# Expert layer in a hybrid decoder step: eight equal expert jobs become four pairs of a 192-slot and a 128-slot job

## The reference

```python
logits = einsum('btd,de->bte', h, w_router) + b_router
top_p, top_i = lax.top_k(softmax(logits), 2)
gates = sum(one_hot(top_i, 8) * (top_p / sum(top_p))[..., None], axis=-2)
for e in range(8):
    y = y + gates[..., e:e+1] * ((silu(h @ wg[e]) * (h @ wu[e])) @ wd[e])
```

## Time and profile before

| | |
|---|---|
| runs | 1703.96 us median of 3 (1699.91 to 1707.03) |
| profiled execution | span 1699.4 us from the first to the last instruction; the page gives no other time of it |
| TensorE busy | 1592.8 us (94%) |
| VectorE, ScalarE, POOL busy | 945.8, 756.0, 540.5 us |
| DMA | 282 MB, mean 166 GB/s |
| expert jobs | eight, from about 1046 to 1678 us of the span |

### The profile page before, as it was taken

The page is one execution under the profiler, slowest core; times in us unless marked ns, Lnnn a source line. Parts: engine busy times, 40 slices in busy tenths (PEclk is TensorE's granted clock), DMA queues, the critical chain, the costliest instruction groups (busy, mean ns, idle before and its releaser), DMA issues.

```text
span 1699.4 us, 29575 instructions
## 1 busy us (share of the span) xinstructions
PE 1592.8 (94%) x11452; PEld 1480.1 (87%) x11452; DVE 945.8 (56%) x1248; ACT 756.0 (44%) x1068; POOL 540.5 (32%) x333
## 2 busy tenths in 40 slices
PE   6998878999999999899888988999999999999998
PEld 5997758999999999898866778989989898989886
DVE  6896554411111000512498349777768686867777
ACT  6444453322222222423586326455545554545455
POOL 1001323254455444143000314614233232415172
PEclk8998879999999999999999998999999999999989
DMA  6624202245444642221764355896969798796961
GB/s 209 132 86 148 83 1 75 73 132 153 128 130 154 199 158 93 68 82 52 255 185 151 105 124 163 284 265 210 298 196 297 198 271 224 234 260 222 257 232 52
DMA packets 346287, 282.01 MB, mean 166 GB/s; under 512 B 9513, under 2 KB 311133, under 8 KB 346071
## 3 DMA queue, kind: packets, MB, share of 16 engines
q1 hardware_dynamic: 324963, 251.09, 50.6%
q10 hardware_dynamic: 18084, 18.14, 3.2%
q0 software_dynamic: 3168, 11.80, 2.4%
HBM read 246.62 MB, written 35.10 MB: 166 GB/s over the span
## 4 chain that ended last, share of the span: by engine, by line
PE 79%; DVE 11%; issue 4%; ACT 4%; DMA 1%; POOL 1%; SPq 1%; ACTq 0%; DVEq 0%; POOLq 0%
PE ps L2452 35%; PE ps L3044 14%; PE ps L3047 6%; PE ps L2438 3%; PE ps L2439 3%; PE ps L2440 3%; PE ps L3071 2%; PE ps L3070 2%; DVE cT L1701 2%; PE ps L2591 2%; DVE wlo L1576 1%; PE ps L2420 1%; DVE ewl L2249 1%; PE ps L2968 1%; PE ps L2477 1%
## 5 line engine op out<-in xcount | busy, mean ns | idle before, releaser
L3044 PE MATMUL ps<-ejx,ewh 128*128 128x384 f32 x1408 | 401.7, 359 | 4.8 <-DVE ejx L2263 1.9
L2249 DVE TENSOR_TENSOR ewl<-eraw,ewh 128x2048 fp32r<-128x2048 f32 (+1 forms) x144 | 304.2, 2113 | 152.8 <-ACT ewh L1418 150.9
L1418 ACT ACTIVATE ewh<-eraw 128x2048 fp32r<-128x2048 f32 (+1 forms) x144 | 255.2, 1773 | 252.7 <-PE ps L3047 145.1
L3047 PE MATMUL ps<-ejx,ewl 128*128 128x192 f32 x1408 | 352.5, 250 | 0.0
L2452 PE MATMUL ps<-hh,whi 128*128 128x260 f32 x1504 | 311.2, 288 | 18.4 <-DVE hl L1951 12.7
L2452 PE MATMUL ps<-hh,wlo 128*128 128x260 f32 x1504 | 306.9, 286 | 0.0
L2452 PE MATMUL ps<-hl,whi 128*128 128x260 f32 x1504 | 306.8, 286 | 0.0
L925 POOL TENSOR_TENSOR ea<-eat,ea 128x128 fp32r<-128x128 f32 x88 | 171.5, 1948 | 340.2 <-ACT ea L1476 339.9
L3044 PEld LDWEIGHTS ps<-ejx,ewh 128*128 128x128 f32 x1408 | 264.2, 188 | 8.4 <-issue 7.0
L3047 PEld LDWEIGHTS ps<-ejx,ewl 128*128 128x128 f32 x1408 | 268.9, 191 | 0.0
L2452 PEld LDWEIGHTS ps<-hh,whi 128*128 128x128 f32 x1504 | 237.1, 192 | 22.0 <-issue 15.9
(11 more groups left out here) (451 smaller groups left out, 2498.5 us busy)
## 6 DMA issues: line engine op xcount, KB each, us to landing
eraw<-in_w_gate_e SPq DMA_DIRECT2D x88, 512.0 KB
eraw<-in_w_up_e SPq DMA_DIRECT2D x88, 512.0 KB
eraw<-in_w_down_e SPq DMA_DIRECT2D x64, 512.0 KB
eraw<-in_w_down_e SPq DMA_DIRECT2D x48, 256.0 KB
xs<-zero ACTq DMA_DIRECT2D x10, 1152.0 KB, 4.8
raw<-in_w_gate_d SPq DMA_DIRECT2D x22, 512.0 KB, 4.0
raw<-in_w_up_d SPq DMA_DIRECT2D x22, 512.0 KB, 5.2
raw<-in_w_down_d SPq DMA_DIRECT2D x16, 512.0 KB, 4.5
```

The costliest lines, as they stand in the source:

```text
L1418: e.activation(ewh[:, s, 0:n], eraw[:, u % RAW, 0:n], ACT.Copy).then_inc(ew_hi, 1)
L2249: e.tensor_tensor(ewl[:, s, 0:n], eraw[:, u % RAW, 0:n], ewh[:, s, 0:n].bitcast(F32), ALU.subtract)\
L3044: e.matmul(ps[:, q, 0:2 * C], ewh[:, s, o:o + P], ejx[:, k, :, :].rearrange("p h n -> p (h n)"), start=(k == 0), stop=(k == KD - 1), skip_ ...
L3047: ins = e.matmul(ps[:, q, C:2 * C], ewl[:, s, o:o + P], ejx[:, k, 0, :], start=False, stop=(k == KD - 1), skip_group_check=True)
```

## The change

The experts are ordered by count. The four largest get "wide" jobs of 192 slots, the four smallest "slim" jobs of 128 slots; a wide and a slim one form a pair, and the slots of a pair are 320 rows of `xs` and `ys`. The loop now runs over pairs. The pair order is wide, slim; the last pair runs slim, wide. If a count exceeds its capacity, more pairs are appended. A wide job works as before. A slim job has the 128 tokens stationary in gate and up too and moves the weights, 256 columns of gate and 256 of up for four k-tiles per unit; its hidden values come out with the tokens on the partitions and are turned by TensorE in six blocks of 256 columns (the last of 128). VectorE makes the low parts of those too (POOL has only the wide jobs' ones). The weights of the first job are loaded once the largest expert is known. Cut to its core:

```diff
-MAXJOBS = (2 * T + E * C) // C
+PAIR = C + P
+BIG = E // 2
+MAXP = BIG + 6
+        LATE = {4: KE - 1, 5: KE}
+        POOL_LOW = ()
+        def turn_block(u):
+            return next((b for b in range(BLOCKS) if u == LATE.get(b, 2 * b + 3)), None)
+        def done_block(u):
+            return u // 2 - 1 if u % 2 == 0 and 2 <= u <= 10 else BLOCKS - 1 if u == KE else None
 # SP: load_expert
+                    if t == WIDE or u == KE - 1:
+                        ...
+                    else:
+                        v = eraw[:, s, :].rearrange("p (k j n) -> p k j n", k=KD // 2, j=2)
+                        k0, c0 = u % 2 * (KD // 2), u // 2 * 2 * P
+                        k1, c1 = k0 + KD // 2, c0 + 2 * P
 # SP: start
-            for u in range(RAW):
-                load_expert(0, u)
-            e.wait_ge(jobs_ready, 1)
+            e.wait_ge(head_ready, PG_END + 1)
+            ex = e.value_load(headi[0:1, 0:1], min_val=0, max_val=E - 1)
+            for u in range(PER_JOB):
+                if u >= RAW:
+                    raw_free(0, WIDE, u, False)
+                load_expert(WIDE, ex, u)
 # ACT
+            def slim_act(j, last=False):
+                for u in range(PER_JOB):
+                    if n0 + u + 2 < PAIR_UNITS:
+                        expert_hi(j, n0 + u + 2, last)
+                    b = done_block(u)
+                    if b is not None:
+                        e.wait_ge(bg_done, j * KE + (PG_END + min(2 * b + 2, KE)))
+                        e.activation(bsg[:, b % 2, 0:w], ps[:, EB[eb_at(b)[0]], 0:w], ACT.Silu).then_inc(bs_silu, 1)
+                    b = turn_block(u - 1)
+                    if b is not None:
+                        e.wait_ge(bt_turned, j * BLOCKS + (PG_END + b + 1))
+                        e.activation(ea[:, 2 * b:2 * b + w // P, 0:P], ps[:, 4 + b % 2, 0:w]..., ACT.Copy).then_inc(bt_hi, 1)
+                    if u == KE + 1:
+                        for c in range(4):
+                            rows_hi(c, j * 8 + (4 * place(SLIM, last) + 4 + c + 1), C)
 # DVE: the largest expert, then its one-hots; behind them the list
+            link(e.scalar_tensor_tensor(out=key, in0=cnt, scalar=float(E), in1=io8[:, 0, :], op0=ALU.mult, op1=ALU.subtract))
+            link(e.tensor_reduce(head[:, 0:1], key, AX, ALU.max))
+            ...
+            e.tensor_scalar(headi[:, :], head[:, 1:2], float(E), None, ALU.add).then_inc(head_ready, 1)
+            ...
+            link(e.tensor_tensor(trij[:, :, :], key.unsqueeze(1)..., key.unsqueeze(2)..., ALU.is_gt))
+            link(e.tensor_reduce(rank, trij[:, :, :], AX, ALU.add))
+            ...
+            e.tensor_copy(sloti[:, :, :], slf[:, :, :]).then_inc(slots_ready, 1)
+            ...
+            e.tensor_copy(jobi[:, 0:2 * MAXP + 1], jobf[:, 0:2 * MAXP + 1]).then_inc(jobs_ready, 1)
 # DVE
+            def slim_dve(j, last=False):
+                for u in range(PER_JOB):
+                    if n0 + u + 2 < PAIR_UNITS:
+                        expert_lo(j, n0 + u + 2, last)
+                    b = done_block(u)
+                    if b is not None:
+                        e.wait_ge(bs_silu, j * BLOCKS + (PG_END + b + 1))
+                        e.tensor_tensor(bt[:, b % 2, 0:w], ps[:, EB[eb_at(b)[0]], w:2 * w], bsg[:, b % 2, 0:w], ALU.mult)\
+                         .then_inc(bt_ready, 1)
+                    b = turn_block(u - 1)
+                    if b is not None:
+                        e.wait_ge(bt_hi, j * BLOCKS + (PG_END + b + 1))
+                        e.tensor_tensor(ea[:, ..., C + CB:2 * C], ps[:, 4 + b % 2, 0:w]..., ea[:, ..., 0:P].bitcast(F32),
+                                        ALU.subtract).then_inc(bt_lo, 1)
+                    if u == 1 and last:
+                        slim_rows(j * 2 + 1, j * 48)
+                    elif u == 1:
+                        wide_rows(j * 2 + 2, j * 48 + 16, j * 2)
+                    if u == KE + 1:
+                        for c in range(4):
+                            rows_lo(c, j * 8 + (4 * place(SLIM, last) + 4 + c + 1), C)
 # PE
+            def turn_hidden(j, b, last):
+                e.wait_ge(bt_ready, j * BLOCKS + (PG_END + b + 1))
+                ...
+                for k in range(block_cols(b) // P):
+                    ins = e.transpose(ps[:, 4 + b % 2, k * P:(k + 1) * P], bt[:, b % 2, k * P:(k + 1) * P], ident[:, :])
+                ins.then_inc(bt_turned, 1)
+            def slim_pe(j, last=False):
+                for u in range(PER_JOB):
+                    split_ready(j, n0, last)
+                    if u < KE:
+                        ...
+                        ks = range(KD) if u == KE - 1 else range(u % 2 * (KD // 2), u % 2 * (KD // 2) + KD // 2)
+                        for i, k in enumerate(ks):
+                            ins = three(ps[:, EB[q], 0:w], ejx[:, k, 0, 0:P], ejx[:, k, 1, 0:P], ewh[:, s, i * w:(i + 1) * w],
+                                        ewl[:, s, i * w:(i + 1) * w], k == 0, k == KD - 1, True)
+                        ins.then_inc(bg_done, 1)
+                    else:
+                        ...
+                            for c in range(2):
+                                ins = three(ps[:, 2 + c, :], ea[:, k, 0:P], ea[:, k, C + CB:2 * C], ewh..., ewl..., ...)
+                    b = turn_block(u)
+                    if b is not None:
+                        turn_hidden(j, b, last)
+                    if u == KE:
+                        wide_rows_in(j * 48 + (32 if last else 48), j)
+            with e.Fori(0, last) as j:
+                wide_pe(j)
+                slim_pe(j)
+            slim_pe(last, True)
+            wide_pe(last, True)
```

More of the change, by code:

```diff
@@ L492, in build, with place, unit_of, job_of @@
         EB_USES = [7, 7, 6, 6]
+        EB_PAIR = [u + 1 for u in EB_USES]
         def eb_at(n):
             return n % 4, n // 4
+        WIDE, SLIM = 0, 1
+        BLOCKS = 6
+        LATE = {4: KE - 1, 5: KE}
+        POOL_LOW = ()
+        PAIR_UNITS = 2 * PER_JOB
+        POOL_UNITS = len(POOL_LOW)
+        DVE_UNITS = PAIR_UNITS - POOL_UNITS
+        assert PAIR_UNITS % RAW == 0 and PAIR_UNITS % SPLIT == 0
+        def place(t, last):
+            return 1 - t if last else t
+        def unit_of(t, u, last):
+            return place(t, last) * PER_JOB + u
+        def job_of(j, t, last):
+            return j * 2 + place(t, last)
+        def kind_at(n, last):
+            return (n // PER_JOB if not last else 1 - n // PER_JOB), n % PER_JOB
+        def low_at(n, last):
+            t, u = kind_at(n, last)
+            if t == SLIM and u in POOL_LOW:
+                return ew_lop, POOL_UNITS, PG_END + POOL_LOW.index(u) + 1
+            before = sum(kind_at(m, last) not in [(SLIM, x) for x in POOL_LOW] for m in range(n + 1))
+            return ew_lo, DVE_UNITS, before + RAW
+        def turn_block(u):
+            return next((b for b in range(BLOCKS) if u == LATE.get(b, 2 * b + 3)), None)
+        def done_block(u):
+            return u // 2 - 1 if u % 2 == 0 and 2 <= u <= 10 else BLOCKS - 1 if u == KE else None
+        def block_cols(b):
+            return 2 * P if b < BLOCKS - 1 else P
+        def wide_use(t, q, last):
+            return 2 if last else 1
         def unit(u):
@@ L920, in _, with slim_low @@
             e.wait_ge(jobs_ready, 1)
-            nj = e.value_load(jobi[0:1, MAXJOBS:MAXJOBS + 1], min_val=E, max_val=MAXJOBS)
+            def slim_low(j, last):
+                for u in POOL_LOW:
+                    n = unit_of(SLIM, u, last)
+                    s = n % SPLIT
+                    e.wait_ge(ew_hi, j * PAIR_UNITS + (n + 1))
+                    e.tensor_tensor(out=ewl[:, s, :], in0=eraw[:, n % RAW, :], in1=ewh[:, s, :].bitcast(F32), op=ALU.subtract)\
+                     .then_inc(ew_lop, 1)
             def rest(j, m):
```

476 lines of the change are left out of this document (311 added, 165 removed).

## The result

The changed kernel takes 1625.64 us, the median of four runs (1623.71 to 1626.09); the kernel before, run on the same chip, takes 1704.28. The ratio is 0.954 (95% interval 0.9525 to 0.9555). Forecast was 1625. The profiled span fell from 1699.4 to 1624.3, by 75.1 us. A span is not a run's time: the runs that list both take 1.7 to 2.1 us more than their span, one kernel's profiled run 2.9.

The account below looks back on a forecast made before the run. TensorE's streamed columns were taken to bound every job. Slim jobs -84.5, wide jobs -1.9 and start +7.2 give -79.2 us; on the median 1703.96 that is 1624.8, forecast 1625, own range 1614 to 1636, 8 in 10 1602 to 1652.

Parts of the forecast that it names:

- The slim job: Each 128-slot job: 58.0 us for the first three, 52.3 for the last, against 77.7 per job before; -84.5 us in all.
- The waits: TensorE's pauses in a slim job: 3.0 us at block 0, 1.3 at block 4, 5.47 minus nothing hidden at its end, 53.4 to 55.4.
- The clock: In each of the first three slim jobs, one fall to half rate behind the 3.0 us gap, losing 2.6 us.
- The last slim job: Runs before its wide job, with only two result copies in front of unit 4, so the 3 us go: 52.3 us.
- Transfers: Slim gate and up weights in 1024-byte runs at 290 to 414 GB/s stay hidden; adjacent slim jobs could lose 2 us, taken as 0.
- Wide jobs: Unchanged, but three of them turn only eight large tiles of the next rows: -0.6 us each, -1.9 in all.
- The start: TensorE's first job begins at 1053.2 instead of 1046.02 us: +7.2, bounds 0 and 10.
- The list: VectorE's job list before the first job: 43 chained operations where there were 7, 0.22 us each, 9.5 us.
- the larger zero fills of xs and ys lie in the dense layer, whose DMA is not full: Before the jobs, in the dense layer: the larger fills were given no time of their own in the sum.
- TensorE alone: Rival, 15%: VectorE and the clock lose nothing, slim jobs 49.2 us each; 1595 to 1613 us.
- The weights' flow: Rival, 28%, shared with VectorE's chain: either binds the whole slim job, 65.1 us at 290 GB/s; 1659, most likely 1637 to 1660.
- A fifth pair: Rival, 4%: counts beyond the capacities make the loop run another wide and slim job, 135 us; 1760 us.

Follow-up runs that it names:

- short units first: The changed kernel with the slim job's seven down units cut 1,1,1,2,2,2,2 k-tiles instead of 2,2,2,2,1,1,1; 1610.36 us.
- few fills: The changed kernel with room for five pairs instead of ten, so smaller zero fills of xs and ys; a single run, 1616.62 us.
- one experiment: The kernel before, with one of the seven chained operations ahead of its job list issued 37 times; 1711.99 us against 1703.67.
- the unedited run: The changed kernel measured once more with no edit, as base for its variants; 1624.94 us, ratio 0.9537.
- the last experiment: The changed kernel with results spread, store later, short down units first, blocks 4 and 5 late, part of list moved, TensorE's first pair ahead of its loop; 1600.26 us.
- the last two experiments: The changed kernel with the combined edits, without and then with TensorE's first pair ahead of its loop; 1605.06 and 1600.26 us.

## Why the prediction was right

**The slim job.** Forecast 3 x 58.0 + 52.3 = 226.3 us; measured 56.93 + 56.73 + 56.77 + 55.44 = 225.9. That the sums meet within 0.4 is partly luck: the first three jobs came out 3.6 us under their forecast together, the last one 3.1 over. The stage from the first job's start to the last job's went from 545.4 us (1046.02 to 1591.44) to 461.3. The mechanism stands: VectorE's order makes the first wait, shown twice, by spreading the operations and by taking one part to POOL; the short last units make the one at the end, shown by their reversal. The waits were forecast at 3.0, 1.3 and 2.0 (53.4 to 55.4; the text also says 1.6), and are 2.69, 1.6 and 2.05. The result operations took 3.85 us (1142.98 to 1146.83), not 4.1; the 256-wide product 0.41, not 0.42.

**The clock.** One fall per slim job was forecast, at 2.6 us. There is one behind each of the three waits at block 0 here, but it gave only about 1.7 us of work away: 3 us at 0.52 and 3 at 0.91 lose 1.44 + 0.27. The pause of 2.05 us, which the prediction put into no term of its own, did the same in some places: at 1326 to 1332, behind one of them, the clock is 0.77 and 0.66. And the fall at block 0 is not certain either: two other profiles have one such pause of 2.63 us each with 1.00 behind it (short units first at 1411.07, few fills at 1281.69). The term of 2.6 us per job was too large by 0.9, and no term stood for the pauses elsewhere.
The Trainium skill (TensorE: Matmul & The Clock Gate, HAM oscillation) says that pauses between bursts put the array back to half rate. The trace agrees behind the 2.69 us pause, at 0.52; one experiment, too, in which a longer wait ahead of the first job gave 0.53. It does not agree behind the two pauses of 2.63 us just named.

**The last slim job** took 55.4 and not 52.3. The result operations did leave its front, as forecast: no wait stands at its block 0. But it holds 3.00 us at block 4. This is the place where the prediction said of the adjacent slim jobs that they "could come short, by 2 us at 290", and then took 0: ScalarE waited 3.8 us for weights there. In the unedited run, without those waits, the job takes 54.0 (1463.24 to 1517.26), 1.7 over the forecast: 0.3 of it at block 4 (1.58 against 1.3), 0.6 at the end (2.17 against 1.6); for the rest there is a stretch at 0.72 from 1464 to 1470, behind the 2.1 us pause at its start.

**Transfers** otherwise as said: from the first job's start on ScalarE waits for no weights but in that job (2.6 us for down weights, 1.2 for up weights). How little there is to spare there shows in the last experiment, where it is 10.4 us. The rate at 1024-byte runs lies between the two known ones: 290, about 350, up to 414 GB/s.
The Trainium skill (DMA: Bandwidth & Descriptors, Specifications) puts line rate from 512 bytes on; the three rates disagree with it.

**Wide jobs.** Forecast -1.9 us in all. Only one shows it: they take 79.26, 76.87 and 79.29 us, where 77.7 - 0.6 = 77.1 was expected. The two long ones begin with a fallen clock: at 1056.47 a 384-column matmul lasts 0.66 us where it has 0.41 in the earlier trace rows, and 1326 is the fall just named, which gives 1.7 us of the 2.4 over 76.87. Together they lie 4.1 us over 231.3. (The kernel before had 79.2 for its first job as well.)

**The start** is the step that failed in size: +10.45 (1056.47 against 1046.02) where +7.2 was forecast. The list gave its part: 43 operations took 9.39 us, not 9.5 (0.218 each; the seven in the trace before give 1.61 / 7 = 0.23 and not the 0.22 of the text, but the estimate held), and from its first operation to the first job it is 22.39 us (22.4 in the unedited run and with few fills, too) instead of 15.6: +6.8. But 3.66 us had been lost before it began, at 1034.08 instead of 1030.42, and 6.5 in the unedited run. The step in the text was "the larger zero fills of xs and ys lie in the dense layer, whose DMA is not full": in the window of 560 to 580 us of the kernel before the DMA share was 1.04 already, and the text had looked at 640 to 660, at 0.27. With fewer fills 2.7 of the 3.66 are gone, and so is the idle time at 570. How a shift of one us there moves the clock's falls 400 us later stays open, and there is one run with few fills.

**The balance.** Forecast for the spans was -79.2, measured -75.1. Stage of jobs: 545.4 - 84.5 - 1.9 = 459.0 us forecast, 461.3 measured, +2.3 (457.9 in the unedited run, -1.1). Start: +3.3. From the last job's start to the end: 106.54 against 107.96, -1.4, forecast at 0. Together +4.1. That last term has a row in the waits of the kernel before, 2.1 us for `esg` in its last job, which is gone; the clock at 0.92 above costs 1.7 us against it in this profile, and in the unedited one, at 1.00, the end is 103.9 us and so 4 shorter. The medians differ by 78.6, 3.5 more than the spans. A span lies some 1.8 us under its run's time, so of the 4.9 us that the prediction found between span and median before only about 3 are the choice of execution; the profiled one after lies 0.45 above its median (1626.09 against 1625.64). The forecast took its -79.2 from the spans and hit the medians' -78.6. So the slim jobs as a whole were well sized, while the hit to one us is luck in part: a start costlier than said, an end cheaper, and a profile of before that lay under its median.

**The rivals.** TensorE alone (1595 to 1613) was wrong for this order of work, but the last experiment, at 1600, lies in its range, with slim jobs of 50.6 us where that rival has 49.2: reordering comes near that bound. The weights' flow does not bind the job as long as it waits for VectorE; it showed in one place of one job, more in the adjacent slim jobs of the last two experiments, and in full when SyncE's store held the queue, where the time (1651.8) came into that rival's range. A fifth pair did not occur.

## What to carry to other kernels

When units on the bound engine get shorter, write down the queue of every engine that feeds it, in order, and ask of each operation that used to be free what stands behind it: six copies in front of one small product cost 8.8 us here, three short units at a job's end 14.6. Before moving an operation later, look for a store or a loop bound that waits for it in another queue: a store ahead of loads turned a gain of 9 us into a loss of 27, a list moved back made TensorE start 3.5 us later, counted from the list's first operation. Where work is moved ahead or filled in elsewhere, read that stretch's DMA share before calling it free.

## What the runs showed that was not expected

- The same pause of 2.05 to 2.1 us was followed by half clock at some job starts and not at others: 0.77 and 0.66 behind 1326.26, 1.00 behind 1192.66, and at the last job 0.92 over 21 us in one execution and 1.00 in the other. The same holds for the 2.63 us at block 0: 0.72 over 6 us in one job, 1.00 in another. That is some 1.7 us more or less per place. Runs of one kernel lie 2.4 us (the changed kernel, four) to 9 us apart (unedited, five); that the falls are the cause of all of it is not shown.
- 1 us more at 570 us came with a clock of 0.89 to 0.93 instead of 0.94 some 400 us later in ten of eleven profiles, and with a list that began 0.8 to 9.6 us later. One removed cause, in one run, is all that speaks for cause and effect.
- With the waits for VectorE gone, two adjacent slim jobs wait for weights: 10.4 us of ScalarE's waits in the second, which takes 54.5 us instead of 50.6.
- POOL's 128x2048 subtraction: 4.60 us with one in a job, a mean of 5.17 with six; VectorE's takes 2.29.
- Chained operations of VectorE on 128x8 tiles cost 0.20 us each (37 in 7.36), those of the mixed list 0.22 (43 in 9.39).
